# Forming the up-weight block sums of a two-level fp32 feed-forward on GpSimd instead of VectorE

## What is computed

```python
h2 = rms_norm_2(x, norm2_w[l])
up = causal_dwconv(h2 @ w_up[l], conv_ffn_w[l], conv_ffn_b[l])
g, val = jnp.split(up, 2, axis=-1)
x = x + (jax.nn.gelu(g) * val) @ w_down[l]
```

## Time and profile before

| | us |
|---|---|
| median of 3 runs (3644.07 to 3655.7) | 3648.81 |
| the profiled execution | 3657.36 |
| its span | 3655.3 |
| in it: up stage, TensorE's first to last product | 2905.3 to 3372.6 |
| down stage | 3372.6 to the end |

### The profile page before, as it was taken

One profiled execution on the slowest core, in us unless ns is written; L12 is line 12 of the kernel. 1 busy time (PEld: TensorE's weight loads), 2 busy tenths in 40 slices (PEclk: granted clock), 3 DMA queues, 4 the chain that ended last, 5 costly groups with the idle time before them and its releaser, 6 DMA issues. The chain is left out here.

```text
span 3655.3 us, 63195 instructions
## 1 busy us (share of the span) xinstructions
PE 3222.6 (88%) x27018; PEld 2689.3 (74%) x27018; DVE 2012.8 (55%) x2899; ACT 1392.1 (38%) x2040; POOL 409.6 (11%) x300
## 2 busy tenths in 40 slices
PE   5599999799987498979799989999676899999888
PEld 3488888688887387947699977777444688888667
DVE  6445464555564441344455534565342588988766
ACT  0443334122221322346344432443354454554333
POOL 0122222000000112220000012311011100000000
PEclk8799999777887699999899999999788999999999
DMA  8122332422220431233321103212111322223633
GB/s 349 36 78 80 127 114 72 135 72 52 58 73 20 181 107 51 77 115 130 107 64 59 45 29 116 84 52 81 64 36 52 115 75 87 83 85 133 242 109 115
DMA packets 180277, 343.87 MB, mean 94 GB/s; under 512 B 11168, under 2 KB 115744, under 8 KB 174368
## 3 DMA queue, kind: packets, MB, share of 16 engines
q1 hardware_dynamic: 156464, 242.31, 19.7%
q0 software_dynamic: 23536, 97.53, 7.8%
HBM read 243.72 MB, written 96.08 MB: 93 GB/s over the span
## 5 line engine op out<-in xcount | busy, mean ns | idle before, releaser
L60 PE MATMUL ev_ps<-h_hi,ev_w_hi 128*128 128x512 f32 (+1 forms) x792 | 288.3, 364 | 37.6 <-POOL ev_w_lo L360 36.4
L61 PE MATMUL ev_ps<-h_lo,ev_w_hi 128*128 128x512 f32 (+1 forms) x792 | 281.0, 355 | 0.0
L62 PE MATMUL ev_ps<-h_hi,ev_w_lo 128*128 128x512 f32 (+1 forms) x792 | 280.9, 355 | 0.0
L60 PE MATMUL ff_ps<-ff_op,ff_w_hi 128*128 128x512 f32 x672 | 263.2, 392 | 7.5 <-DVE ff_op L3312 7.2
L61 PE MATMUL ff_ps<-ff_op,ff_w_hi 128*128 128x512 f32 x672 | 262.1, 390 | 0.0
L62 PE MATMUL ff_ps<-ff_op,ff_w_lo 128*128 128x512 f32 x672 | 261.9, 390 | 0.0
L60 PEld LDWEIGHTS ev_ps<-h_hi,ev_w_hi 128*128 128x128 f32 x792 | 150.3, 190 | 76.2 <-POOL ev_w_lo L360 37.2
L2905 ACT ACTIVATE ma_e<-ma_s,ma_nm 128x1280 f32<-128x1280 f32 x64 | 84.9, 1327 | 215.9 <-DVE ma_nm L2939 215.9
L60 PE MATMUL ff_ps<-ff_w_hi 128*128 128x512 f32 x336 | 136.7, 407 | 34.4 <-DVE ff_w_lo L3388 34.4
L61 PEld LDWEIGHTS ev_ps<-h_lo,ev_w_hi 128*128 128x128 f32 x792 | 150.4, 190 | 21.8 <-issue 1.7
L62 PEld LDWEIGHTS ev_ps<-h_hi,ev_w_lo 128*128 128x128 f32 x792 | 150.2, 190 | 21.2
(11 more groups left out here) (542 smaller groups left out, 8554.6 us busy)
## 6 DMA issues: line engine op xcount, KB each, us to landing
w_up_raw<-in_w_up SPq DMA_DIRECT2D x48, 512.0 KB, 4.6
w_up_raw<-in_w_down SPq DMA_DIRECT2D x48, 512.0 KB, 4.3
ev_w<-in_ev_w_in POOLq DMA_DIRECT2D x33, 512.0 KB, 3.9
ada_wt<-in_ada_w POOLq DMA_DIRECT2D x12, 1024.0 KB, 8.2
ada_wt<-in_ada_w SPq DMA_DIRECT2D x12, 1024.0 KB, 8.3
ffn_mid<-h POOLq DMA_DIRECT2D x24, 512.0 KB, 2.9
ff_mem<-ffn_mid SPq DMA_DIRECT2D x24, 512.0 KB, 10.6
ar<-ev_ar SPq DMA_DIRECT2D x8, 1280.0 KB, 5.7
```

The source lines that it names most:

```text
L60: nc.tensor.matmul(out, w_hi, x_hi, start=start, stop=False, skip_group_check=resumed)
L61: nc.tensor.matmul(out, w_hi, x_lo, start=False, stop=False, skip_group_check=resumed)
L62: return nc.tensor.matmul(out, w_lo, x_hi, start=False, stop=stop, skip_group_check=resumed)
```

## The change

The four sums of every pair are taken out of VectorE's list and put into GpSimd's, with the same operands, waits and counts. GpSimd forms the sums of pairs 0, 1 and 2 ahead of its first store; from then on the four sums of pair u+2 stand directly ahead of the store of middle tile u, and so behind the store of tile u-1.

```diff
 @block.gpsimd
 def _(pool):
-    for u in range(NU):
-        pool.wait_ge(prod, u + 1)
-        pool.dma_start(g.mid[u], acc[u % 2][1]).then_inc(mid_stored[u % 2], 16)
+    def add(u, j):
+        s = 2 * (u % 2)
+        if u >= 2:
+            for half in range(2):
+                pool.wait_ge(loaded[s + half], 16 * (u // 2))
+        if u:
+            pool.wait_ge(w_lo_done, PROD * (u - 1) + j + 1)
+        a11, a12, a21, a22 = raw[:, s, first], raw[:, s, second], raw[:, s + 1, first], raw[:, s + 1, second]
+        if j in (2, 5):
+            pool.wait_ge(combos, 4 * u + S_AT[j])
+        x0, x1, op = {1: (a21, a22, ALU.add), 4: (a11, a21, ALU.subtract), 2: (e[:, 0], a11, ALU.subtract), 5: (a12, e[:, 1], ALU.subtract)}[j]
+        nc.gpsimd.tensor_tensor(e[:, {1: 0, 2: 1, 4: 2, 5: 3}[j]], x0, x1, op).then_inc(combos, 1)
+
+    for u in range(NU + 2):
+        if u < NU:
+            for j in (1, 4, 2, 5):
+                add(u, j)
+        if u >= 2:
+            pool.wait_ge(prod, u - 1)
+            pool.dma_start(g.mid[u - 2], acc[u % 2][1]).then_inc(mid_stored[u % 2], 16)
...
 @block.vector
-                add(0, 1)
-                add(0, 4)
...
-                    if more:
-                        add(u + 1, 1)
-                        add(u + 1, 4)
...
-                        add(u + 1, 2)
...
-                        add(u + 1, 5)
```

More of the change, by code:

```diff
@@ L3291, in _ @@
                 tt, stt = nc.vector.tensor_tensor, nc.vector.scalar_tensor_tensor
[L3293 to L3304, removed]
                 def lo(u, j):
@@ L3399, in _ @@
                 lo(0, 0)
-                add(0, 1)
-                add(0, 4)
                 t_lo(T1)
                 lo(0, 1)
-                add(0, 2)
                 t_lo(T2)
@@ L3407, in _ @@
                 lo(0, 3)
-                add(0, 5)
                 t_lo(T3)
```

## The result

The changed kernel is slower by half a per cent. Its median is 3661.91 us of 13 runs (3650.63 to 3674.75), that of the kernel before, run beside it, 3642.97 us of 13 (3632.29 to 3655.7). The ratio is 1.0053, with a 95% interval of 1.0038 to 1.0067: 14 to 24 us more.

What follows compares the result with a forecast made beforehand. TensorE, busy throughout the up stage, was taken to bound the kernel. Start gain -1.8 plus stalls +5.5 gave +3.7 us on the median 3648.8: forecast 3652.5, range 3642 to 3670.

Steps and rivals of the forecast that it cites:

- a longer stall: Rival, chance 0.26: GpSimd's sums run half a microsecond later, both scalings behind sums; 0.78 us a pair, +14.6, 3663.4 us.
- VectorE's removed work buys nothing in steady pairs: Steady up-stage pairs: VectorE loses 2.4 us a pair, none of it on TensorE's path.
- The start gives 1.8 us: Start of the up stage: ScalarE's two stops for VectorE sums (1.24 and 0.54 us) go, P6 starts 1.8 us earlier.
- Exclusion of GpSimd additions and VectorE operations with two SBUF inputs, not of corners: Up stage: such operations exclude each other; one reading PSUM and one SBUF tile isn't held.
- Alternation, the one waiting goes next: Between VectorE and GpSimd: the operation already waiting goes next; a waiting GpSimd sum ends 1.19 us after VectorE's operation.
- s2: GpSimd's third sum of a pair (j = 2): waits, ends at 3125.76, with the first row scaling queued behind it.
- s5: GpSimd's fourth sum of a pair (j = 5): waits, ends at 3128.02; the second row scaling ends 1.65 us late.
- s1 waits for it: Behind the store: GpSimd's first sum waits for VectorE's split of j = 4 and ends at 3122.79.
- The stall of 0.26 a pair: P6 in pairs 3 to 23: TensorE waits for `keep(p1)` behind the late second scaling; 21 x 0.26 = +5.5 us.
- The room of 1.38: Second scaling through second tap and `keep(p1)` to P6: 0.14 + 1.24 = 1.38 us of lateness costs nothing.
- chain half a microsecond later: Bound: GpSimd's chain starts 0.5 us later, order kept; second scaling 2.15 us late, stall 0.78 us a pair.
- Stores later in order, not in time: Middle-tile stores behind the sums: each is issued where it was, at no cost.

Runs made afterwards that it cites:

- the link cut: Changed kernel with ScalarE's `keep(p1)` put ahead of the second tap: 3639.94 us against 3643.67 for the kernel before, ratio 0.9987.
- the early `keep`: Kernel before, sums on VectorE, with only pair 0's `keep(p1)` moved up ahead of `t_hi(T4)`: 3637.88 us against 3644.0, ratio 0.9982.
- dummy additions: Kernel before, VectorE keeping its sums, plus four GpSimd additions 21 times, writing a tile nobody reads: one run, 3698.88 us beside 3647.77.
- memsets: Kernel before plus four GpSimd memsets of a 128x512 tile at the same places, reading no SBUF: one run, 3648.27 us beside 3647.77.
- the order forced: Changed kernel with GpSimd's first sum of a pair waiting for the split of j = 4, like its second: 3650.15 us, ratio 1.0022.

## Why the prediction was right or wrong

The range, 3642 to 3670, held the 3661.91, and the time came out on the rival "a longer stall" (3663.4), not on the forecast of 3652.5 with its 0.70 for no measurable change. That the two numbers agree to 1.5 us is in part luck: the forecast stood on 3648.8 for the kernel before, whose median beside this one was 3642.97. As a change it was +3.7 for the forecast and +14.6 for that rival, against 18.9 in the medians and 16.5 in the stage. The mechanism was right, the size of one term was not.

- **VectorE's removed work buys nothing in steady pairs**: right. With the link cut, stores are 19.04 us apart, with 2.4 us less work on VectorE a pair.
- **The start gives 1.8 us**: right in cause, somewhat small. From the first product to P6 it is 11.9 us (2896.5 to 2908.36) instead of 14.2, so 2.3. Some 0.3 of it is no gain: the first product itself begins later, its split held by a sum (1.10 instead of 0.69). The wait is 3.85, not 5.4, since P1 and P5 end 0.7 and 1.1 us later after the first product's start. P5 starts as a held split ends (2899.67 + 1.78 = 2901.45, P5 at 2901.50), and P1's first matmuls ran at the lower clock (0.63), as they did in the kernel with only the early `keep`. That the wait is `keep(p1)`'s is shown by the early `keep`. The slow matmuls behind the wait stayed, as the prediction had put them: 0.50 of the clock from 2909.7 to 2912.7.
- **Exclusion of GpSimd additions and VectorE operations with two SBUF inputs, not of corners**: right, with the dummy additions and memsets.
- **Alternation, the one waiting goes next**: right for the second, third and fourth sum. s2, begun at 3121.98 behind the split, ends 1.15 after it (1.19 assumed); s5 ends 1.15 after the first scaling (3122.29 + 2.31 = 3124.60). An addition that waits for the one before it begins 0.17 later, not 0.30; nothing hung on that.
- **"s1 waits for it"** is the step that failed. The sum directly behind the store went ahead of the split of j = 4, though the split's row begins 0.37 us earlier. The second sum, which needs that split, came behind it: it ended 4.21 us after `multiply` instead of 3.64, 0.57 late, and everything behind it is late by as much, 0.51 to 0.57.
- **The stall of 0.26 a pair, 5.5 us in all**, is the mis-sized term. Measured 0.88 x 21 = 18.5. Of the difference of 0.62, 0.54 is the second scaling, 2.19 late where I had 1.65, and that lateness is there from the second sum on, so it is the order of the first sum and no error in the later swaps. The other 0.08 is mostly TensorE's restart, which I had left out. With the order forced the stall is 0.59 and not 0.26, because the wait that forces it makes the second sum 0.27 late by itself (it ends 3.91 us after `multiply`); a kernel that has my order without such a wait was not run.
- **The room of 1.38** and the bound "chain half a microsecond later", 2.15 late and 0.78 of stall, met the changed kernel's 2.19 and 0.88. Its half microsecond was a guess that came out, with another cause: the chain was not late in an unchanged order, its first two members had changed places. What was wrong was to hold that case for the less likely one: nothing in the rows of before showed an addition directly behind a store, and I gave the open case 0.26.
- **Stores later in order, not in time**: right; each follows its `multiply` by 0.29 us, as before. **Sum**: -2.3 + 18.5 = 16.2, measured in the stage 16.5.

## What to carry to other kernels

Work moved to GpSimd beside a busy VectorE wasn't beside it at all here, where both read two SBUF operands: price it as VectorE time of GpSimd's length, at the moment when it runs, and then follow the first in-order link from there to the engine that bounds. A hold costs nothing if such links have room, and here a reordering of two ScalarE instructions gave that room. Where a profile names a releaser, check it against the counts in the code; here moving one copy earlier, without any of the offload, won as much as that and the reordering did in the changed kernel, as far as the intervals tell.

## What the hardware showed that I had not expected

- An addition on GpSimd directly behind a DMA issue holds VectorE before its own row begins: the split begun at 3118.12 was held by an addition recorded from 3118.49, while in the kernel where that addition waits for the split, the same split beside the same store ran its 0.69. The store alone doesn't hold. The Trainium skill (Perfetto Trace Analysis, GPSIMD Engine Instruction) warns that recorded spans on this engine are unreliable. These rows fit that. What exactly is taken early, no run shows.
- A stop of TensorE of 1.98 us, in the kernel with dummy additions, was followed about 0.8 us after its end (3103.07) by matmuls of 0.63 instead of 0.39 us. But stops as long in the same kernel, of 1.97 us ahead of 3081.77 and 1.98 ahead of 3146.41, were not, so the length of a stop alone doesn't tell. After those of 1.13 us there, and after the 0.60 of the changed kernel, the matmuls kept 0.39 to 0.40.
- The same program part ahead of the changed stage ended between 2887.1 and 2906.9 us in the profiled runs, more than what the change costs. For differences of this size the stage's own time is the better measure.
